# One written order of sixteen rounds for the mixer of the second block, and GpSimd for its masks and diagonals

## The reference

```python
def hybrid_mixer(h, w_in, gate_bias, g_q, g_k, g_mh, w_out):
    proj = (h @ w_in).astype(jnp.float32)
    mq, mk, mv, mo, mg, aq, ak, av = jnp.split(proj, idx, axis=-1)
    ...
    hm = bidirectional_mlstm(heads(mq, M_HEADS), heads(mk, M_HEADS) * (M_QK_DIM ** -0.5), heads(mv, M_HEADS),
                             gates[0], jax.nn.log_sigmoid(gates[1]), gates[2], jax.nn.log_sigmoid(gates[3]))
    hm = rms_norm(hm.transpose(0, 2, 1, 3), g_mh.reshape(M_HEADS, M_V_DIM))
    hm = (hm * jax.nn.sigmoid(mo.reshape(B, S, M_HEADS, M_V_DIM))).reshape(B, S, M_HEADS * M_V_DIM)
    ...
    ha = dilated_attention(qa, ka, heads(av, A_HEADS))
    ...
    return jnp.concatenate([hm, ha], axis=-1).astype(h.dtype) @ w_out

def dilated_attention(q, k, v):
    outs, lses = [], []
    for w, d in zip(WINDOWS, DILATIONS):
        o, l = dilated_band_attention(q, k, v, d, w // (2 * d))
        ...
    wts = jax.nn.softmax(jnp.stack(lses), axis=0)
    return jnp.sum(wts[..., None] * jnp.stack(outs), axis=0)
```

## Time and profile before

| | us |
|---|---|
| median of three runs (3206.55 to 3207.32) | 3207.26 |
| the profiled execution | 3206.36 |
| its span | 3204.4 |

### The profile page before, as it was taken

The page is one execution under the profiler, slowest core; times in us unless marked ns, Lnnn a source line. Parts: engine busy times, 40 slices in busy tenths (PEclk is TensorE's granted clock), DMA queues, the critical chain, the costliest instruction groups (busy, mean ns, idle before and its releaser), DMA issues.

```text
span 3204.4 us, 37150 instructions
## 1 busy us (share of the span) xinstructions
PE 3104.4 (97%) x15012; PEld 2517.3 (79%) x15022; DVE 1905.7 (59%) x2786; ACT 1042.2 (33%) x1525; POOL 9.7 (0%) x23
## 2 busy tenths in 40 slices
PE   8999999998899999999999999999999998899998
PEld 7888888786678888788877888878887765578887
DVE  7876654636665555666657555466665565564434
ACT  4212222435442222422235222332223435442222
POOL 0000000000000000000000000000000000000000
PEclk9999999999999999999999999999999998899999
DMA  6433342210033443256532353235451220133231
GB/s 228 144 119 119 137 146 79 65 52 11 2 125 132 143 173 124 82 178 233 187 117 71 131 186 130 87 115 190 169 215 57 79 66 1 47 121 103 92 99 53
DMA packets 102964, 369.19 MB, mean 115 GB/s; under 512 B 11358, under 2 KB 12638, under 8 KB 102540
## 3 DMA queue, kind: packets, MB, share of 16 engines
q1 hardware_dynamic: 101788, 362.14, 33.2%
q0 software_dynamic: 1008, 4.69, 0.4%
HBM read 364.69 MB, written 2.10 MB: 114 GB/s over the span
## 4 chain that ended last, share of the span: by engine, by line
PE 86%; DVE 8%; ACT 4%; issue 1%; DMA 1%; SPq 0%; POOL 0%; DVEq 0%; ACTq 0%; POOLq 0%
PE ps L193 25%; PE ps L195 24%; PE ps L194 24%; PE ps L197 4%; PE ps L198 2%; DVE SQ L615 1%; DVE HL L604 1%; DVE WL L185 1%; PE ps L2869 1%; DVE XT L1038 1%; DVE RAW L1501 0%; DVE DUMP L306 0%; ACT WH L180 0%; DMA STG<-in_w_modt 0%; PE ps L500 0%
## 5 line engine op out<-in xcount | busy, mean ns | idle before, releaser
L193 PE MATMUL ps<-HH,WH 128*128 128x512 f32 x2400 | 947.2, 395 | 5.4 <-ACT S L915 2.2
L195 PE MATMUL ps<-HH,WL 128*128 128x512 f32 x2400 | 936.4, 390 | 0.0
L194 PE MATMUL ps<-HL,WH 128*128 128x512 f32 x2400 | 936.0, 390 | 0.0
L180 ACT ACTIVATE WH<-RAW 128x1024 fp32r<-128x1024 f32 x456 | 459.0, 1048 | 630.9 <-PE ps L195 361.8
L185 DVE TENSOR_TENSOR WL<-RAW,WH 128x1024 fp32r<-128x1024 f32 x456 | 542.7, 1219 | 75.3 <-ACT WH L180 75.1
L193 PEld LDWEIGHTS ps<-HH,WH 128*128 128x128 f32 x2400 | 450.9, 188 | 111.3 <-issue 10.2
L195 PEld LDWEIGHTS ps<-HH,WL 128*128 128x128 f32 x2400 | 450.9, 188 | 96.8
L194 PEld LDWEIGHTS ps<-HL,WH 128*128 128x128 f32 x2400 | 451.2, 188 | 95.7 <-issue 3.8
L1038 DVE SCALAR_TENSOR_TENSOR XT<-ps,DER,XT 128x512 f32<-128x512 f32 x512 | 346.6, 683 | 246.5 <-PE ps L195 231.7
L193 PE MATMUL ps<-GH,WH 128*128 128x512 f32 x1056 | 414.1, 392 | 4.8 <-DVE GL L946 4.8
L195 PE MATMUL ps<-GH,WL 128*128 128x512 f32 x1056 | 411.1, 389 | 0.0
(11 more groups left out here) (373 smaller groups left out, 2600.0 us busy)
## 6 DMA issues: line engine op xcount, KB each, us to landing
RAW<-in_w_modt SPq DMA_DIRECT2D x200, 512.0 KB, 5.0
RAW<-in_ffn_wi SPq DMA_DIRECT2D x182, 512.0 KB, 4.9
RAW<-in_w_gu SPq DMA_DIRECT2D x90, 512.0 KB, 4.5
RAW<-in_ffn_wo SPq DMA_DIRECT2D x88, 512.0 KB, 4.7
RAW<-in_w_in SPq DMA_DIRECT2D x44, 512.0 KB, 3.6
RAW<-in_w_down SPq DMA_DIRECT2D x44, 512.0 KB, 3.9
RAW<-in_w_out SPq DMA_DIRECT2D x16, 512.0 KB, 4.4
STG<-in_w_modt SPq DMA_DIRECT2D x10, 512.0 KB, 12.9
```

The lines of the kernel that those rows point to most:

```text
L180: act.e.activation(u.hi, u.ld.view, ACT.Copy).then_inc(u.hi_done.sem, 1)
L193: pe.e.matmul(out, wh, x[0], start=first, stop=False)
L194: pe.e.matmul(out, wh, x[1], start=False, stop=False)
L195: m = pe.e.matmul(out, wl, x[0], start=False, stop=last)
```

## The change

`mlstm` and `dilated` are replaced by one function, `rounds`, that adds the steps of both parts in sixteen written rounds: in round r one mLSTM unit (h, j = r // 4, r % 4) and one dilated round, with `DilCount`, `DilTrans`, the PV product and the mLSTM sum of earlier rounds between. `MlExp` is cut in two, `MlWeights` (ScalarE) and `MlScore` (TensorE), so that the weights stand ahead of the dilated exponentials in ScalarE's queue. A has six slots instead of four. The additions of `MlMask` and the diagonal products of `DilDen` move from VectorE to GpSimd, with a semaphore of their own; the reciprocal stays on VectorE. Each of the next head's masks is asked for at the end of the round of block 3. Q and K of the second pair of heads are split in rounds 2 and 3. The use of bank 3 for transposes at the end is dropped. The order of the output products changes from dilated slices with the mLSTM's in between to 4, 5, 6, 0, 1, 7, 2, 3.

```diff
-        self.afree = {s: NONE for s in range(4)}
+        self.afree = {s: NONE for s in range(6)}
...
-        self.A = sb("A", [128, 4, T])
+        self.A = sb("A", [128, 6, T])
...
-        self.done = [m.P.s["ml_dve"].next() for _ in range(2)]
+        self.done = [m.P.s["ml_pool"].next() for _ in range(2)]
         m.mask[h] = self
 
-    def vector(self, dve):
+    def gpsimd(self, pool):
...
         for d in range(2):
-            dve.wait_ge(*m.bcast[h, d])
-            dve.wait_ge(*self.free[d])
+            pool.wait_ge(*m.bcast[h, d])
+            pool.wait_ge(*self.free[d])
...
-            dve.e.tensor_tensor(m.MD[d].rearrange("p (n t) -> p n t", t=128),
+            pool.e.tensor_tensor(m.MD[d].rearrange("p (n t) -> p n t", t=128),
...
-class MlExp(Step):
+class MlWeights(Step):
...
-            s = m.na % 4
+            s = m.na % 6
...
+class MlScore(Step):
+    def __init__(self, m, x):
+        self.m, self.h, self.j = m, x.h, x.j
+        self.qkfree = m.qkfree
+        x.qk = m.P.s["ml_mm"].next()
+        self.done = x.qk
...
 class DilDen(Step):
...
-        self.diag = [s["dil_den"].next() for _ in range(2)]
+        self.diag = [s["dil_diag"].next() for _ in range(2)]
...
         dve.e.reciprocal(w.DEN[:, s, :], w.DEN[:, s, :]).then_inc(self.inv.sem, 1)
-        dve.wait_ge(*self.inv)
-        dve.wait_ge(*self.dfree)
+
+    def gpsimd(self, pool):
+        w, s = self.w, self.j % 2
+        pool.wait_ge(*self.inv)
+        pool.wait_ge(*self.dfree)
         for par in range(2):
-            dve.e.tensor_tensor(w.D[:, 2 * par:2 * par + 2, :].rearrange("p r (h t) -> p r h t", t=128),
+            pool.e.tensor_tensor(w.D[:, 2 * par:2 * par + 2, :].rearrange("p r (h t) -> p r h t", t=128),
...
-            self.side_by_side(self.mlstm(m, w, mix, a["w_out_2"]), self.dilated(w, mix))
+            self.rounds(m, w, mix, a["w_out_2"])
...
+    def rounds(self, m, w, mix, w_out):
...
+        mixed = lambda k, ready: self.add(MixSplit(self, mix, [k], [ready]))
+        unit, last, den, quot, square, root, out = {}, {}, {}, {}, {}, {}, {}
+        split(0, True)
+        split(0, False)
         self.add(MlFloor(m))
...
+        self.add(MlMask(m, 0))
+        for r in range(16):
+            h, j = r // 4, r % 4
+            if r:
+                self.add(DilCount(w, r - 1))
+            unit[r] = self.add(MlWeights(m, h, j))
+            self.add(DilScore(w, r))
+            if r:
+                self.add(DilTrans(w, 2 * r - 2))
+            if h and j == 1:
+                quot[h - 1] = self.add(MlQuot(m, den[h - 1]))
+            self.add(MlScore(m, unit[r]))
+            if r:
+                self.add(DilTrans(w, 2 * r - 1))
+            if r == 1:
+                self.add(MlTurnFloor(m))
+            if h and j == 3:
+                out[h - 1] = self.add(MlOut(m, root[h - 1]))
+            if r > 1:
+                self.add(DilPV(w, r - 2))
+            if r:
+                last[r - 1] = self.add(MlSum(m, unit[r - 1]))
+            self.add(MlProd(m, unit[r]))
+            if h and j == 0:
+                den[h - 1] = self.add(MlDen(m, last[r - 1]))
+                self.add(DilDen(w, h - 1))
+            if h and j == 1:
+                square[h - 1] = self.add(MlSquare(m, quot[h - 1]))
+                self.add(DilQuot(w, h - 1))
+            if h and j == 2:
+                root[h - 1] = self.add(MlRoot(m, square[h - 1]))
+                mixed(3 + h, w.quot[h - 1].done)
+            if r in (2, 3):
+                split(1, r == 2)
+            if j == 3 and h < 3:
+                self.add(MlMask(m, h + 1))
+        self.add(DilCount(w, 15))
+        last[15] = self.add(MlSum(m, unit[15]))
+        self.add(DilTrans(w, 30))
+        den[3] = self.add(MlDen(m, last[15]))
         self.new_ring()
         self.units = self.split([w_out[0]])
...
+        self.add(DilTrans(w, 31))
+        self.add(DilPV(w, 14))
+        quot[3] = self.add(MlQuot(m, den[3]))
+        self.add(DilDen(w, 3))
+        self.add(DilPV(w, 15))
+        square[3] = self.add(MlSquare(m, quot[3]))
+        self.add(DilQuot(w, 3))
+        for k in range(2):
+            mixed(k, out[k].done)
+        root[3] = self.add(MlRoot(m, square[3]))
+        mixed(7, w.quot[3].done)
+        out[3] = self.add(MlOut(m, root[3]))
+        mixed(2, out[2].done)
+        mixed(3, out[3].done)
```

More of the change, by code:

```diff
@@ L2497, in __init__ @@
             self.off.append(m.P.s["ml_act"].next() if o.stop > o.start else self.diag[d])
-        self.qkfree = m.qkfree
-        self.qk = m.P.s["ml_mm"].next()
         m.unit[h, j] = self
@@ L2527, in tensor @@
         pe.e.matmul(m.P.banks[0], m.KH[r, p, js], m.QL[r, p, :], start=False, stop=False)
-        pe.e.matmul(m.P.banks[0], m.KL[r, p, js], m.QH[r, p, :], start=False, stop=True).then_inc(self.qk.sem, 1)
+        pe.e.matmul(m.P.banks[0], m.KL[r, p, js], m.QH[r, p, :], start=False, stop=True).then_inc(self.done.sem, 1)
 class MlProd(Step):
@@ L3749, in mixer_hybrid @@
         return [self.over]
-    def mlstm(self, m, w, mix, w_out):
+    def rounds(self, m, w, mix, w_out):
         m.qsplit, m.ksplit = {}, {}
-        def split(p):
-            for x, hi, lo, splits in ((m.Q, m.QH, m.QL, m.qsplit), (m.K, m.KH, m.KL, m.ksplit)):
-                splits[p] = self.add(HiLo(self, x[:, p, :], hi[:, p, :], lo[:, p, :], []))
-        before, den, quot, square, root, out = [None] * 4 + [{}, {}]
-        split(0)
-        self.add(MlFloor(m))
-        yield
-        for h in range(5):
-            if h == 1:
-                split(1)
-            if h < 4:
-                self.add(MlMask(m, h))
-            for j in range(4):
-                if h and j == 1:
-                    quot = self.add(MlQuot(m, den))
-                x = self.add(MlExp(m, h, j)) if h < 4 else None
-                if h and j == 1:
-                    square = self.add(MlSquare(m, quot))
-                yield
-                if before:
-                    before = self.add(MlSum(m, before))
-                    if j == 0:
-                        den = self.add(MlDen(m, before))
-                if h and j == 2:
-                    root = self.add(MlRoot(m, square))
-                if x:
-                    self.add(MlProd(m, x))
-                before = x
-                if h + j == 0:
-                    self.add(MlTurnFloor(m))
-                yield
-                if h and j == 2:
-                    out[h - 1] = self.add(MlOut(m, root))
-                    if h == 4:
-                        w.ptfree[3] = quot.done
-                        for k in range(4):
-                            yield
-                            self.add(MixSplit(self, mix, [k], [out[k].done]))
@@ new lines, in split @@
+        def split(p, query):
+            x, hi, lo, splits = (m.Q, m.QH, m.QL, m.qsplit) if query else (m.K, m.KH, m.KL, m.ksplit)
+            splits[p] = self.add(HiLo(self, x[:, p, :], hi[:, p, :], lo[:, p, :], []))
+        mixed = lambda k, ready: self.add(MixSplit(self, mix, [k], [ready]))
+        unit, last, den, quot, square, root, out = {}, {}, {}, {}, {}, {}, {}
+        split(0, True)
+        split(0, False)
+        self.add(MlFloor(m))
+        self.add(MlMask(m, 0))
[34 more added lines that the diff above has]
+                self.add(MlMask(m, h + 1))
@@ L3793, in mlstm @@
+        self.add(DilCount(w, 15))
+        last[15] = self.add(MlSum(m, unit[15]))
+        self.add(DilTrans(w, 30))
+        den[3] = self.add(MlDen(m, last[15]))
         self.new_ring()
         self.units = self.split([w_out[0]])
-        yield
-    def dilated(self, w, mix):
-        last = len(w.pairs)
-        for q in range(last + 2):
-            if 1 <= q <= last:
-                self.add(DilCount(w, q - 1))
-            if q < last:
-                self.add(DilScore(w, q))
-                yield
-            if 1 <= q <= last:
-                self.add(DilTrans(w, 2 * q - 2))
-                yield
-                if q % 4 == 0:
-                    self.add(DilDen(w, q // 4 - 1))
-                self.add(DilTrans(w, 2 * q - 1))
-            if q >= 2:
-                self.add(DilPV(w, q - 2))
-                if q % 4 == 1:
-                    self.add(DilQuot(w, q // 4 - 1))
-                yield
-                if q % 4 == 1:
-                    self.add(MixSplit(self, mix, [q // 4 + 3], [w.quot[q // 4 - 1].done]))
+        self.add(DilTrans(w, 31))
```

2 lines of the change are left out of this document (1 added, 1 removed).

## The result

The changed kernel takes 3211.5 us (median of 20 runs, 3207.4 to 3216.7) against 3205.5 us before (20 runs, 3201.5 to 3209.9). The ratio is 1.0019, with a 95% interval of 1.0013 to 1.0025: it is slower, by 6 us, where 7.9 us less were forecast. The profiled execution took 3210.4 us with a span of 3208.2, against 3206.4 and 3204.4 before.

The account below looks back on a forecast made before the run. Waiting in line, no full engine, was taken to bound the second mixer's attention stage. 2662 + 94.5 + 2.4 + 14 + 2.5 = 2775.4 against 2783.3, 7.9 us less: 3199.4 from a median of 3207.3, range 3192 to 3212.

Parts of the forecast that it names:

- What bounds the stage: Second block's attention stage, 152.3 us: no engine full, waiting in line sets the pace; TensorE idle about 34 us.
- Rounds at full clock: Rounds 4 to 15 replayed as 7.3, 8.7, 7.5 and 8.0 us per head, three times 31.5, or 94.5 us.
- The tail's 14 us: After round 15: last sum, products, quotient, diagonals and transposes take 14 us before the output products start.
- one fall in three heads, 2.4 us: TensorE's clock drops to 1.2 GHz once in rounds 4 to 15, at a j=1 wait of 1.8 us, costing 2.4.
- the steady 1.56 us: TensorE's idle time ahead of the second transposes in a steady round; claimed to hold the clock.
- rival B: VectorE's two-input work and GpSimd's stop each other at head changes: 3211 with half, 3223 in full; chance 0.25.
- six places at 4 us (24): Cost of VectorE held by one GpSimd operation (1.57), plus a clock fall (2.4), at two places per head change.
- GpSimd's duration: A 128x512 mask addition or diagonal product on GpSimd takes 1.57 us, range 0.52 to 1.57.
- The masks' wait, the slots, the start: GpSimd masks cost nothing up to 2.5 us each; A's slots cost nothing; round 1 starts at 2637.2 as before.
- Rival C: Waits shift and eat the gain: replayed rounds 0.5 us longer in practice, 6 us over twelve, 3205; chance 0.13.
- D: GpSimd far slower than its memset: at 5 us each, masks and tail cost 22 us, 3221; chance 0.05.
- E: The change does less than it says: the tail stays as long as before, 3207; chance 0.02.

Follow-up runs that it names:

- late_fill_all: Changed kernel with GpSimd's masks and diagonals delayed, overwritten score-matmul repeats from round 2 on, filler matmuls before the first score and in the tail; 3188.3 us, ratio 0.9946.
- late: Changed kernel plus one wait ahead of GpSimd's masks and diagonals, so they run beside VectorE operations reading one SBUF operand; ratio 0.9989 to the kernel before.
- late_slots4: Changed kernel with GpSimd's work delayed and A at four slots instead of six; profiled once, no ratio, stage 143.5 us.
- write_only: Changed kernel with each GpSimd addition or product replaced by three memsets of the same tile; profiled once, no ratio, stage 149.3 us.

## Why the prediction was wrong, point by point

*What bounds the stage* was read rightly: waits in line, not a full engine, and the long rounds at the end of the old order. The new order removed them.

*Rounds at full clock.* The replay's 7.3, 8.7, 7.5 and 8.0 were measured as 7.28, 8.54, 7.55 and 7.81 in *late_fill_all*. The tail's 14 us were 12.8. One sum is off: a start at 2637.2 and rounds of 8.9, 7.5 and 7.5 us put round 4 at 2661.1, not 2662.

*The clock* is the step that failed first: the term "one fall in three heads, 2.4 us". The text took rows with 1.37 and 1.73 us of idle time, behind which the transposes were still at 2.4 GHz, for a bound that clears the steady 1.56 us. In the changed kernel waits of 1.48 to 1.57 us let the clock fall each time (five of five), and 1.20 to 1.22 never (five of five). Of the steady rounds only j=0 had so short a wait, 1.20 to 1.22 instead of the 1.56 replayed; j=2 had 1.48 to 1.50. Two things were wrong in the reading. The rows of before stood singly among other work, while here they come once a round: the kernel before held the clock even behind 1.57 us in its round 5, as the PV product shows.

```profile
2678.69 0.63 PE L2839 MATMUL ps<-K,PP 128*128 128x128 f32 x4 [1.57 <-ACT PT L2846]
2679.25 1.09 PE L2869 MATMUL ps<-PT,DVt 128*64 128x128 f32 x16
```

And the text looked at the transposes right behind the wait; the row that tells is the one after them. In round 6 of the changed kernel the transposes take 0.72 us, which still looks warm, and the PV behind them 1.98. A fall cost 1.56 us (9.11 against 7.55), not 2.4, but there were eight in rounds 4 to 15, not one; six are left without the lock. From *late* to *late_fill_all* the stretch from round 4 on went from 115.6 to 106.1 us: 9.5 us for the clock, where 2.4 stood in the sum.

*GpSimd beside VectorE* is the second step that failed: the sum had nothing for it. It was rival B, with a chance of 0.25 and its mechanism and most of its places as they came. Its price: round 3 is 2.7 us longer (10.0 against 7.28), and from round 4 on it is 122.7 against 115.6, together 9.7 us; in that are the clock falls that the lock brings with it in rounds 3 and j=3. The text's six places at 4 us (24) was too much, since VectorE was held by 1.07 us, not by a whole 1.57 each time, and since the falls in j=1 came anyway. I weighed it too low by an argument without a row, that VectorE may start first and finish. One of three operations did.

*GpSimd's duration* was inside its bounds: 1.53 and 1.34 with the lock, 1.27 and 1.04 without. The estimate of 1.12 for an addition was nearer than the 1.57 that the sum took.

*The masks' wait, the slots, the start*: costed at nothing, and nothing was measured for the slots (*late_slots4*). The mask at the start wasn't late. Round 3, though, was forecast at 7.5 and is 10.0, since the second head's masks meet its counts.

The terms close. The replayed stage had 140.8 us and the measured one 153.4. The lock adds 9.7 us and the clock 7.1 over its 2.4; the rounds at full clock and the tail came 2.4 us shorter, and rounds 0 to 3, without the lock's 2.7, 1.9 shorter. That makes 153.3.

By the text's own bound of 0.2%, the measured 6 us are just inside "within 0.2%". But the whole interval lies above 1, so the sign of the forecast was wrong. On the 3207.3 us that the forecast started from, 1.0019 makes 3213.4: above the range's end of 3212, and 2.4 us above where half of rival B stood. That the measured median itself, 3211.5, lies under 3212 is luck: the median of the kernel before came out 1.8 us lower in its 20 runs than in the three that the forecast started from.

Rival C, rounds longer in practice than replayed, named the direction, but not the size (1.3 us a round instead of 0.5) and not the reason: with lock and falls gone the rounds are no longer than replayed. D and E did not come: no wait on GpSimd is seen on ScalarE in mid-stage, and the long last rounds are gone.

## What to carry to other kernels

When an elementwise operation moves from VectorE to GpSimd, ask what VectorE runs at that moment. If it reads two SBUF operands and GpSimd reads SBUF, both engines pay. A wait that puts GpSimd's work beside row maxima or PSUM operands can be faster than no wait, as it was here (0.9989 against 1.0019).

A regular schedule repeats its wait in each round, so a wait of 1.5 us that did no harm once can cost the clock nearly every time. Look at the second row behind a wait for the clock, not at the first. If the wait can't be removed, matmuls into a bank that is overwritten can hold the clock, but only where the chain has room, and its gain may stay only after the other delay is gone: the same fill was worth nothing beside the lock in the heads where masks follow, and 3.1 us a head without it.

## What the runs showed of the hardware that I had not expected

GpSimd's additions of 128x512 took 1.27 us alone and up to 1.73 beside VectorE's two-operand operations, and these took 1.76 instead of 0.68. Three memsets on GpSimd at the same time left them at 0.68.

TensorE's clock mostly fell after waits of some 1.5 us and mostly held after 1.2 us, but not always. In the twelve traces of the written order, behind waits of 1.43 to 1.57 us ahead of the second transposes it fell 31 times and held 5 times, and behind 1.20 to 1.24 us it held 47 times and fell 11 times. In *write_only* it went the other way round in each head: a round with a wait of 1.46 us took 8.55 us, and the round ahead of it, with 1.22, took 8.89. So the length of one wait alone doesn't decide. What else does wasn't tried.

At the start of the stage the same instructions ran at the lower clock for more or fewer rounds in different executions (28.0 or 32.4 us for rounds 0 to 3), which is a part of the 8 to 9 us by which runs of one kernel differ.
